# Four weight slabs of the last mixer loaded by two transfers each, of 88 and of 40 partitions

## What is computed

```
for l in range(2):
    h = rms_norm(x, norm1_g[l])
    proj = h @ w_in[l]
    ... forgetting attention, convolution, recurrence ...
    x = x + mixed @ w_out[l]
    h2 = rms_norm(x, norm2_g[l])
    x = x + peer(h2, peer_wq[l], peer_k1[l], peer_k2[l], peer_u[l], peer_v[l])

hid = gelu(einsum("td,tkd->tk", xi, u_tab[ei]))
out = einsum("tk,tkd->td", gi * hid, v_tab[ei])
```

## Time and profile before

| | |
|---|---|
| Median of 3 runs | 2036.84 us (2034.08 to 2039.52) |
| The profiled execution, its own time | 2033.49 us |
| Span, first to last instruction | 2031.7 us |
| PE (matmul), busy | 1696.1 us, 83% |
| DVE, busy | 1370.9 us, 67% |
| ACT, busy | 839.6 us, 41% |
| POOL, busy | 590.8 us, 29% |
| Bytes moved | 770.12 MB, mean 379 GB/s |
| Gathers (q0), slabs and other plain loads (q1) | 536.90 and 231.85 MB |
| Slab transfers of 1024 KB on the ring | 200, median 9.2 us from issue to landing |
| Gathers | 512, median 20.4 to 20.7 us from issue to landing |

### The profile page before, as it was taken

How to read it: one execution, slowest core, us unless ns; L and a number is a source line. 1 busy time by engine, 2 the same in 40 slices (tenths; PEclk the granted TensorE clock), 3 DMA queues, 4 the chain that set the end, 5 groups by cost and what they waited for, 6 DMA issues and landing times.

```text
span 2031.7 us, 21349 instructions
## 1 busy us (share of the span) xinstructions
PE 1696.1 (83%) x6956; PEld 970.8 (48%) x6956; DVE 1370.9 (67%) x3575; ACT 839.6 (41%) x2112; POOL 590.8 (29%) x517
## 2 busy tenths in 40 slices
PE   9999999999889889886779888877887897765555
PEld 4459866673477374372236435422553462211111
DVE  4324336478766388686876776887777688877776
ACT  2423214434488137423443463345347334432222
POOL 0000000020422324423443343334433434345441
PEclk9999999999999999898999989999999999987777
DMA  9687878579999999999999999999999999999995
GB/s 389 213 320 252 300 247 270 171 266 376 414 419 419 420 419 420 419 418 420 420 420 419 419 402 419 419 420 420 420 420 406 416 419 419 420 420 420 420 418 232
DMA packets 108384, 770.12 MB, mean 379 GB/s; under 512 B 12144, under 2 KB 12656, under 8 KB 16368
## 3 DMA queue, kind: packets, MB, share of 16 engines
q0 software_dynamic: 73728, 536.90, 64.0%
q1 hardware_dynamic: 34544, 231.85, 29.9%
HBM read 767.65 MB, written 1.05 MB: 378 GB/s over the span
## 4 chain that ended last, share of the span: by engine, by line
DMA 42%; PE 37%; ACT 7%; DVE 6%; issue 6%; POOL 2%; SPq 0%; DVEq 0%; POOLq 0%; ACTq 0%
DMA arena<-in_peer_dram,eidx 16%; PE psum L1138 9%; DMA ring<-in_peer_dram,eidx 8%; DMA ring<-in_slabs_dram 8%; PE psum L752 7%; PE psum L775 7%; DMA kv<-in_peer_dram,eidx 7%; PE psum L977 6%; PE psum L994 3%; DMA early<-in_peer_dram,eidx 3%; ACT diag L1470 1%; ACT wexp L1463 1%; DVE arena L2042 1%; ACT L1460 1%; DVE x L2052 1%
## 5 line engine op out<-in xcount | busy, mean ns | idle before, releaser
L2195 POOL DMA_INDIRECT arena<-in_peer_dram,eidx x204 | 233.0, 1142 | 799.3 <-DVE eidx L1914 428.2
L1460 ACT ACTIVATE wexp<-wexp 128x1 f32<-128x1 f32 x512 | 103.1, 201 | 698.0 <-DVE wexp L2042 696.8
L1138 PE MATMUL psum<-arena,diag 128*128 128x512 f32 x592 | 301.4, 637 | 65.0 <-ACT diag L1470 64.7
L2042 DVE CUSTOM_DVE_ANT_0 arena<-arena,osb 128x1024 f32<-128x1024 f32 x204 | 248.8, 1221 | 113.2 <-DMA arena<-in_peer_dram,eidx 112.0
L1138 PE MATMUL psum<-ring,diag 128*128 128x512 f32 x448 | 233.2, 647 | 74.6 <-ACT diag L1470 74.3
L2195 POOL DMA_INDIRECT ring<-in_peer_dram,eidx x154 | 176.9, 1149 | 317.8 <-PE psum L1138 275.6
L752 PE MATMUL psum<-ring,hT 128*128 128x512 f32 x560 | 256.2, 606 | 9.9 <-DMA ring<-in_slabs_dram 8.2
L1138 PE MATMUL psum<-kv,diag 128*128 128x512 f32 x316 | 177.5, 690 | 80.1 <-ACT diag L1470 79.7
L2042 DVE CUSTOM_DVE_ANT_0 ring<-ring,osb 128x1024 f32<-128x1024 f32 x154 | 187.8, 1221 | 62.1 <-DMA ring<-in_peer_dram,eidx 61.0
L1138 PEld LDWEIGHTS psum<-arena,diag 128*128 128x128 f32 x592 | 110.7, 200 | 224.2 <-ACT diag L1470 124.4
L1138 PEld LDWEIGHTS psum<-ring,diag 128*128 128x128 f32 x448 | 84.3, 201 | 199.4 <-ACT diag L1470 120.0
(11 more groups left out here) (333 smaller groups left out, 2125.7 us busy)
## 6 DMA issues: line engine op xcount, KB each, us to landing
ring<-in_slabs_dram SPq DMA_DIRECT2D x200, 1024.0 KB, 9.2
ring<-in_slabs_dram SPq DMA_DIRECT2D x8, 768.0 KB, 4.3
kept<-in_slabs_dram SPq DMA_DIRECT2D x4, 1024.0 KB, 13.0
arena<-in_peer_dram,eidx POOLq DMA_INDIRECT x204, 20.5
ring<-in_peer_dram,eidx POOLq DMA_INDIRECT x154, 20.7
ring<-in_slabs_dram SPq DMA_DIRECT2D x4, 512.0 KB, 4.9
kk<-in_keys_dram SPq DMA_DIRECT2D x2, 1024.0 KB, 8.7
kv<-in_peer_dram,eidx POOLq DMA_INDIRECT x103, 20.4
```

The source lines that it names most:

```text
L1138: ins = pe.matmul(bank(b), diags_of(n), pair(slot_of[n])[:, 1024 + 512 * h:1536 + 512 * h], start=(k == 0), stop=(k == 127))
L1460: act.activation(wn, wn, ACT.Gelu_apprx_tanh).then_inc(*up("gelu", n))
L2042: v.tensor_tensor_reduce(out=row, in0=row, in1=row_y[t], scale=1.0, scalar=0.0, op0=ALU.mult, op1=ALU.add, accum_out=wexp[:, c:c + 1]).the ...
L2195: pool.indirect_dma_start(pair(i), None, tables, bass.IndirectOffsetOnAxis(ap=eidx[:, 128 * t + k:128 * t + k + 1], axis=0)).then_inc(sig. ...
```

## The change

The first four slabs that M11 takes are each loaded by two transfers into the same place of the ring, partitions 0 to 87 and 88 to 127, one behind the other. Both add 16 to the same semaphore, so `filled` counts such a slab twice, and TensorE waits for both. Bytes, places and the order of the slabs are as before; the planner does not see the cut.

```diff
@@ -24,6 +24,7 @@
 PAIR = 2048
 SLOT = 2048
 NRING, NLATE = 6, 3
+CUT, CUT_SLABS = 88, 4
 LAG = 3
 
 START, MERGE, NORM, LAST, MIX = (8, 9), (5, 2), (18, 2), 5, (16, 2, 3, 2, 4)
@@ -341,8 +342,12 @@
         def before(n):
             return n - NRING if n < less[0] else n - NLATE
 
+        def cut():
+            return [n for n, s in enumerate(takes) if s == "M11"][:CUT_SLABS]
+
         def filled(n):
-            return sum(place(m) == place(n) for m in range(n + 1))
+            in_two = cut()
+            return sum(2 if m in in_two else 1 for m in range(n + 1) if place(m) == place(n))
 
         def slot(n):
             return ring[:, place(n) * SLOT:(place(n) + 1) * SLOT]
@@ -2207,7 +2212,9 @@
                 count[0] += 1
                 if n >= NRING:
                     w.wait_ge(*at(*consumed.get(before(n), ("ffn_down", 1, 10))))
-                sp.dma_start(slot(n)[:, 0:width], T["slabs"][i][:, 0:width]).then_inc(sig.sem("slab%d" % place(n)), 16)
+                ends = (0, CUT, P) if n in cut() else (0, P)
+                for a, b in zip(ends, ends[1:]):
+                    sp.dma_start(slot(n)[a:b, 0:width], T["slabs"][i][a:b, 0:width]).then_inc(sig.sem("slab%d" % place(n)), 16)
 
             def small(l):
```

## The result

The kernel became **slower**: median 2062.24 us (2061.06 to 2063.67, 4 runs) against 2036.92 us (2034.08 to 2039.52, 4 runs), a ratio of 1.0125 with a 95% interval of 1.0107 to 1.0142, or +25.3 us. The forecast was -7.2 us, and the time lies far outside its range. The profiled execution after took 2061.71 us (span 2059.9), 28.2 us more than that of before.

What follows compares the result with a forecast made beforehand. Transfers were taken to bound the gather stretch, one late DMA engine the end. Freed engines -10.0 us, loaded ones +5.0; the typical loaded engine then ends last, -7.2 us: 2036.84 to 2029.6 us, range 2025.0 to 2038.5.

Steps and rivals of the forecast that it cites:

- The bet on which engine is late: At the last gathers: the engine finishing last is among five the cut relieves, -7.2 us; chance 0.66.
- the late engine: One DMA engine of 16, 10 to 12 us behind the others at the end, pacing all gathers at 2.49 us.
- rival 1: Last gathers: the slow engine is among ten given more rows; 5.0 us slower, 2041.8 us; chance 0.20.
- the freed five: Engines 11 to 15, given no rows of a split slab: 2.50 us less work per slab, -10.0 us over four.
- the loaded ten: Engines given 12 rows instead of 8 per split slab: 1.25 us more each, +5.0 us over four.
- the coarsest rival: Split slabs dealt in coarser shares, eight engines at 16 rows instead of 8: 10.0 us slower, 2046.8 us.
- Rival 2: Whole kernel: rows spread evenly, slow engine's load unchanged, or gain lost to PE and DVE waits; 2036.8 us; chance 0.14.
- the issues on SyncE: Four added slab issues, 1.3 us together, on an engine that mostly waits; claimed to cost nothing.
- the fourth slab's margin: Slab issued at 1438.0 us lands 5.9 us before its read; the split's 2.8 us delay is covered.
- a tail of 0.06 at the end: Last windows: DMA share of one engine alone; if still there and 5 us longer, the slow engine was loaded.
- a *share* that sinks under 1.0: DMA share over longer stretches after 1290 us; would mean the gain was spent on waits for PE.

Runs made afterwards that it cites:

- 64/64: Kernel before with the same four slabs each loaded as partitions 0 to 63 and 64 to 127: 2051.86 us, ratio 1.0077.
- the second run: Kernel before plus spare late loads, mostly of every fourth partition, some packed: four spread partitions, six times, cost 1.9 us; no whole-kernel time given.
- The probes: Kernel before plus spare loads nobody reads, among the last gathers, priced by how far dots move: 0 to 127 cost 2.48 us, 0 to 87 5.26.

## Why the prediction was wrong

It put the time at 2029.6 us; it was 2062.24. Against the forecast of -7.2 us the change cost +25.3, 32.5 us off, in two steps.

1. **The bet on which engine is late: "I bet that such a service burden is put at the far end from where transfers are counted."** This failed: the late engine is the fourth in the dealing, loaded with 4 more rows per slab, 16 x 0.312 = 5.0 us, which is rival 1's price. From -7.2 to +5.0 are 12.2 us of the error. It had no row behind it and was given 0.66; a bet without a row, between ten engines loaded, five freed and one left as it was, would have been 5 in 16 for "freed". The Trainium skill's rule that engines 7 and 15 are usually slower ("DMA: Bandwidth & Descriptors", "Latency and other measured facts") does not hold here either: counted as the transfers are dealt, from the lowest number up, the late one is number 3.
2. **The part that costed a slab by "rows per engine" alone.** "Per slab the freed five lose 2.50 us of work and the loaded ten gain half of that" takes 0.312 us per row for granted, whatever partitions a transfer covers. That was never bounded: the price of a transfer of part of the partitions was an operation that the trace did not show, and only its dealing was bounded, not its speed. A cut slab costs 6.14 us more than a whole one, of which 1.25 are the late engine's rows and 4.9 the crowding. For four slabs the crowding is 19.6 us, where 20.3 of the error are left to explain, and it is the whole reason why the time lies above even the coarsest rival, 2046.8.

Rival 2, nothing moves, fell too. The Trainium skill's advice in the same page's "Rules for kernel authors", against two transfers for two halves of the partitions because they serialize, is borne out, but the prediction's reading of it, that the time would stay the same, is not: 64/64 costs 16.8 us. The time does stay for halves that are cut so that both reach all ports, +0.6 us.

What held: the stretch is bound by transfers, and what is lost at 1262 to 1308 us is still missing 700 us later at the end; one late engine sets the pace of all landings, 2.49 us each; 88 and 40 rows are dealt over eleven and ten engines (5 more packets per cut slab, 34564 against 34544 in all); the issues on SyncE and the fourth slab's margin cost nothing. The sign that the text named for rival 1, a tail of 0.06 at the end, was there; "longer by 5 us" was not, as it has the same length and stands later. And it named what would make it wrong, a *share* that sinks under 1.0: the share did not sink, the rate did.

No version beat the kernel before. The late engine gets a row from every transfer that is dealt over four engines or more, and the two splits that cost nothing gained nothing.

## What to carry to other kernels

Where transfers set the pace, load all 128 partitions in one transfer, and if one must be split, split by columns or by every second partition: those were free here, while 64/64 in neighbouring halves cost 4.0 us per MB and 88/40 6.1. Read the DMA share and the GB/s side by side: a share of 1.0 at 245 instead of 419 GB/s was, here, engines that were all busy but wrote to too few places, and no wait shows it as such. Before betting on which of several like units is the slow one, measure it, or give each one its even chance.

## What was unexpected

- Neighbouring partitions: 24 rows of 8 KB into four of them cost 7.6 us, about 0.31 us each, as if one at a time, though four engines carried them (5.5 and 7.7 in the second run); into four partitions spaced by four, 24 rows cost 1.9.
- A crowded transfer slows the packets of other queues on the same engines: gathers that landed after 24 to 34 us took 40 to 55, and their median packet 548 ns instead of 313.
- It needs no other traffic: 219 instead of 415 GB/s for slabs in halves of 64 alone at the start.
- One engine is some 10 us behind the others at the end of the kernel before and of the changed one. The probes put it fourth in the dealing, clearly in one run (partitions apart) and in agreement with it in another, on a different chip.
